# A macaron decoder layer: two more q/k products by Strassen's scheme, and wider transfers for each attention head

## The reference

```
h = x + 0.5 * SwiGLU_1(rmsnorm(x))
u = rmsnorm(h)
[xp | q | k | v | gate_logits] = u @ w_in       # 512 | 512 | 512 | 512 | 2048 columns
y_pool = causal_pool_mixer(xp) @ w_branch_pool  # 4 groups of 128 channels, windows 2, 4, 8, 16
y_sb = stick_breaking_attention(q, k, v) @ w_branch_attn   # 8 heads of 64, no softmax
m = sigmoid(g_pool) * y_pool + sigmoid(g_sb) * y_sb
h = h + m @ w_out
h = h + 0.5 * SwiGLU_2(rmsnorm(h));  out = rmsnorm(h)
```

## Time and profile before

| | |
|---|---|
| runs | 1937.56, 1937.66, 1938.7 us (median 1937.66) |
| profiled execution, first to last instruction (span) | 1937.1 us; the median is 0.56 us above it |
| busy PE / PEld / DVE / ACT / POOL | 1923.7 / 1607.4 / 1338.3 / 772.0 / 136.9 us |
| mean granted PE clock | 0.999 of full speed |
| mean DMA rate | 179 GB/s |

### The profile page before, as it was taken

How to read it: one execution, slowest core, us unless ns; L and a number is a source line. 1 busy time by engine, 2 the same in 40 slices (tenths; PEclk the granted TensorE clock), 3 DMA queues, 4 the chain that set the end, 5 groups by cost and what they waited for, 6 DMA issues and landing times.

```text
span 1937.1 us, 25171 instructions
## 1 busy us (share of the span) xinstructions
PE 1923.7 (99%) x9094; PEld 1607.4 (83%) x9094; DVE 1338.3 (69%) x1656; ACT 772.0 (40%) x1154; POOL 136.9 (7%) x218
## 2 busy tenths in 40 slices
PE   9999999999999999999999999999999999999998
PEld 9888888888888888888888888888888888888887
DVE  6987777775566667425777778789767776755655
ACT  7423232333434424214565652464323232324344
POOL 1000000000000100002333320010000000000002
PEclk9999999999999999999999999999999999999999
DMA  5456645468676503546645347643535454677665
GB/s 163 148 202 229 226 160 164 171 219 309 201 237 194 179 24 103 177 152 190 164 131 161 108 148 249 206 143 109 183 132 187 149 184 139 221 262 241 206 192 204
DMA packets 245092, 347.20 MB, mean 179 GB/s; under 512 B 16144, under 2 KB 150032, under 8 KB 240400
## 3 DMA queue, kind: packets, MB, share of 16 engines
q1 hardware_dynamic: 245008, 346.09, 54.9%
HBM read 232.79 MB, written 112.98 MB: 178 GB/s over the span
## 4 chain that ended last, share of the span: by engine, by line
PE 55%; DVE 2%; DMA 1%; issue 1%; ACT 1%; SPq 0%; POOL 0%; POOLq 0%; DVEq 0%; ACTq 0%
PE bank L1091 20%; PE bank L1188 12%; PE bank L1135 4%; PE bank L1137 4%; PE bank L1136 4%; PE bank L1047 2%; PE bank L1257 2%; PE bank L1285 2%; PE bank L1349 2%; DMA dn_lo_raw<-act_dram 1%; PE bank L1366 1%; PE bank L1365 1%; PE bank L1336 1%; PE bank L1334 1%; DVE tail_p L2471 0%
## 5 line engine op out<-in xcount | busy, mean ns | idle before, releaser
L1905 DVE TENSOR_TENSOR dn_lo<-dn_lo_raw,dn_hi 128x1024 fp32r<-128x1024 f32 x149 | 181.8, 1224 | 151.6 <-ACT dn_hi L1545 151.2
L1091 PE MATMUL bank<-hi_t,wa_hi 128*128 128x512 f32 x640 | 249.1, 389 | 0.2 <-issue 0.2
L1091 PE MATMUL bank<-hi_t,wa_lo 128*128 128x512 f32 x640 | 249.0, 389 | 0.0
L1091 PE MATMUL bank<-lo_t,wa_hi 128*128 128x512 f32 x640 | 249.0, 389 | 0.0
L1545 ACT ACTIVATE dn_hi<-dn_lo_raw 128x1024 fp32r<-128x1024 f32 x149 | 158.0, 1061 | 217.6 <-DMA dn_lo_raw<-act_dram 217.6
L1135 PE MATMUL bank<-dn_hi 128*128 128x512 f32 x596 | 232.7, 390 | 0.6 <-DVE dn_lo L1905 0.6
L1136 PE MATMUL bank<-dn_hi,dn_lo 128*128 128x512 f32 x596 | 231.9, 389 | 0.0
L1137 PE MATMUL bank<-dn_lo,dn_hi 128*128 128x512 f32 x596 | 231.9, 389 | 0.0
L1091 PE MATMUL bank<-hi_b,wa_hi 128*128 128x512 f32 x480 | 186.9, 389 | 0.5 <-DVE up L2029 0.5
L1091 PE MATMUL bank<-lo_b,wa_hi 128*128 128x512 f32 x480 | 186.8, 389 | 0.0
L1091 PE MATMUL bank<-hi_b,wa_lo 128*128 128x512 f32 x480 | 186.7, 389 | 0.0
(11 more groups left out here) (237 smaller groups left out, 3555.3 us busy)
## 6 DMA issues: line engine op xcount, KB each, us to landing
wa_lo_raw<-in_ffn_w_gate_up_dram SPq DMA_DIRECT2D x87, 512.0 KB, 5.0
dn_lo_raw<-act_dram SPq DMA_DIRECT2D x149, 256.0 KB, 4.3
act_dram<-g SPq DMA_DIRECT2D x44, 512.0 KB, 4.5
wd_t<-in_ffn_w_down_dram SPq DMA_DIRECT2D x44, 512.0 KB, 6.6
act_dram<-s_of SPq DMA_DIRECT2D x88, 256.0 KB, 6.5
wd_dram<-wd_t SPq DMA_DIRECT2D x22, 1024.0 KB, 6.0
dn_lo_raw<-wd_dram SPq DMA_DIRECT2D x85, 256.0 KB, 3.3
dn_lo_raw<-in_ffn_w_down_dram SPq DMA_DIRECT2D x64, 256.0 KB, 3.0
```

The source lines that it names most:

```text
L1091: last = nc.tensor.matmul(acc, lhs, rhs, start=n == 0 and i != 2 and i < 5, stop=n == 11, skip_group_check=True)
L1905: return nc.vector.tensor_tensor(dst, raw, hi.bitcast(f32), ALU.subtract)
```

## The change

Q and k of head pairs 0 and 1 and both xp units are now made by seven products of 12 matmuls each, in `mix_unit(b)`, in place of four banks of 24. Q and k of pairs 2 and 3 stay as `unit_quad`. All six stand at the front, in the order q/k pair 2, pair 3 (plain), then q/k pair 0, pair 1, xp unit 1, xp unit 0 (mixed units 0 to 3). Values, group products and pool branch follow, and attention comes straight behind the pool branch. The activation sums of the scheme (`tu_*`, four blocks of 128 x 2048) are made once, from `u_hi + u_lo`. The mixed units have their own weight buffers, of which the raw one (`ws_raw`) is single. Q and k go out by a ring of three buffers, 512 KB each for hi and lo. The pool branch's c22 now comes before c11 in unit 0. Its `pool_weight_sums(2)` moves from before c12(0) to after c21(0). A head is loaded by three transfers of 128 rows, and head 0 in two halves of 512 columns. In attention the PSUM banks are renumbered, and `HEAD_SHARE` gives the first step 16 more of the gate matmuls' shares; per step they are [22, 22, 15, 10, 4, ...], before [7, 23, 15, 11, 4, ...], the first 11 ahead of the first logits. Three semaphores are merged into others, the load of ScalarE's sigmoid table moves to before the q/k units, and `down(1)` waits for its banks one pass later.

```diff
+MIX_UNITS = (tuple(("qk", pair) for pair in PAIR_ORDER[2:]) + ... + (("xp", 1), ("xp", 0)))
+HEAD_SHARE = 16
+    shares[0] += HEAD_SHARE
 # PE
+            def mix_unit(b):
+                s = (b + 1) % 2
+                for i in range(7):
+                    place, hi, lo, (kind, slot) = PRODUCTS[i]
...
+                    if b >= 2 and i == 0:
+                        pe.wait_ge(mb_copied, 2 * (b - 2) + 2)
+                    if b >= 2 and i in (1, 3, 4):
+                        pe.wait_ge(mb_add, 5 * (b - 2) + (1 if i == 1 else i + 1))
+                    if i % 2 == 0:
+                        pe.wait_ge(mb_lo, mix_order(b, i // 2))
+                    if b == 0 and i in (2, 3, 4, 6):
+                        pe.wait_ge(rt_lo, {2: 1, 3: 2, 4: 3, 6: 4}[i])
+                    if i == 2:
+                        pe.wait_ge(mb_copied, 2 * b + 1)
+                    if i >= 5:
+                        pe.wait_ge(mb_add, 5 * b + i - 3)
+                    for n in range(12):
...
+                    last.then_inc(mb_prod, 1)
             for m in range(2):
-                unit_quad(U_P[m], U_P[m] % 2, Q_P[m], fresh=m == 0)
+                unit_quad(U_A[m], U_A[m] % 2, Q_A[m], fresh=m == 0)
+            for b in range(NM):
+                mix_unit(b)
+            values(0, range(4))
+            values(1, range(2))
             group_quad(0)
-            values(0, range(NT))
-            values(1, range(4))
+            values(1, range(2, 4))
+            values(0, range(4, NT))
             group_quad(1)
             values(1, range(4, NT))
             for u in range(KT // 2):
                 pool_branch_unit(u)
-            for m in range(4):
-                unit_quad(U_QK + m, (U_QK + m) % 2, Q_QK + m)
 # PE, pool_branch_unit: product 1 runs its six matmuls with w_hi first
-                pe.wait_ge(wlo, U_B + u + 1)
-                        kt, p = n // 3, n % 3
+                        kt, p = (n % 2, n // 2) if i == 0 else (n // 3, n % 3)
+                        if i == 0 and n == 4:
+                            pe.wait_ge(wlo, U_B + u + 1)
 # SP
+            def load_mix(b):
+                if b:
+                    sp_.wait_ge(mb_lo, 4 * b)
...
+            load_mix(1)
+            for b in range(NM - 2):
+                load_mix(b + 2)
+                spill_mix(b, 0)
+                spill_mix(b, 1)
 # SP, load_head
-                for dst, part, cols in ((q_st[top], 0, 0), (q_st[low], 1, 0), (k_hi2[top], 0, SEQ),
-                                        (k_hi2[low], 0, SEQ), (k_lo2[top], 1, SEQ), (k_lo2[low], 1, SEQ)):
-                    sp_.dma_start(dst[:, slot, :].bitcast(f32),
-                                  qk_dram[part, pair, rows, cols:cols + SEQ]).then_inc(head_in[slot], 16)
+                for c0, c1 in ((HALF, SEQ), (0, HALF)) if hn == 0 else ((0, SEQ),):
+                    landed = head_in[slot] if c0 == 0 else half_in
+                    if hn == 0 and c0:
+                        for i in range(3):
+                            sp_.wait_ge(ring_sp[i], 32 * ring_uses(i))
+                        sp_.wait_ge(pool_prod, 6 * (KT // 2 - 1) + 3)
+                    for dst, part in ((k_hi2, 0), (k_lo2, 1)):
+                        sp_.dma_start(dst[:, slot, c0:c1].bitcast(f32),
+                                      qk_dram[part, pair, rows, SEQ + c0:SEQ + c1].unsqueeze(0).broadcast_to([2, 64, c1 - c0])).then_inc(landed, 16)
+                    if hn == 0 and c0:
+                        sp_.wait_ge(pool_prod, 6 * (KT // 2 - 1) + 4)
+                    sp_.dma_start(q_st[:, slot, c0:c1].bitcast(f32), qk_dram[:, pair, rows, c0:c1]).then_inc(landed, 16)
 # DVE
+            def mix_unit(b):
+                if b:
+                    mix_c21(b - 1)
+                    mix_out(b - 1, 1, 0, 4)
+                mix_c11(b)
+                mix_out(b, 0, 0, 1)
+                mix_c22(b, 0)
+                if b + 1 < NM:
+                    mix_weight_sums(b + 1)
+                mix_c22(b, 1)
...
+            split(U_V[0] % 2, U_V[0] + 1, None)
+            mix_c21(NM - 1)
...
             for u in range(KT // 2):
-                if u == 0:
+                if u:
+                    split_static(U_B + u + 1)
                     pool_c11(u)
-                split_static(U_B + u + 1)
-                if u:
+                    pool_c22(u)
+                else:
+                    pool_c22(u)
                     pool_c11(u)
-                pool_c22(u)
-                if u + 2 < KT // 2:
+                    split_static(U_B + u + 1)
+                if u and u + 2 < KT // 2:
                     pool_weight_sums(u + 2)
                 pool_c12(u)
                 pool_c21(u)
+                if u == 0:
+                    pool_weight_sums(u + 2)
 # GpSimd
+            mix_raw(1)
...
+            mix_raw(0)
```

More of the change, by code:

```diff
@@ L90, with tile_of, ring_uses @@
 HEADS = 2 * len(PAIR_ORDER)
+MIX_UNITS = (tuple(("qk", pair) for pair in PAIR_ORDER[2:]) + tuple(("gate", j) for j in range(0, EARLY, 2))
+             + (("xp", 1), ("xp", 0)))
+NM = len(MIX_UNITS)
+FIRST_TILE = 4
+RING_TILES = FIRST_TILE + 2 * (NM - 2)
+RING_AT = tuple((RING_TILES - 1 - i) % 3 for i in range(3))
+RING_LAST = tuple(RING_AT.index(i) for i in range(3))
+def tile_of(b, a):
+    return FIRST_TILE + 2 * b + a
+def ring_uses(slot, before=RING_TILES):
+    return len(range(slot, before, 3))
 def attention_tiles():
@@ L443, in macaron_layer @@
         ms_sum = sem("ms_sum")
-        late_in = [sem(f"late_in{i}") for i in range(3)]
         part_ok = sem("part_ok")
@@ L558, in pool_place @@
         def pool_place(u, b):
-            return pst_odd[:, :] if b == 0 and u % 2 else pst[:, b, :]
+            return pst_even[:, :] if b == 0 and u % 2 == 0 else pst[:, b, :]
         @block.sync
@@ L627, in load_dn @@
                 own = which and e >= LATE
-                into = late_in[e - LATE] if own else dn_in[slot]
+                into = ring_sp[e - LATE] if own else dn_in[slot]
                 if SLOTS <= e and not own:
@@ L1256, in branch_sum @@
                     kt, p = n // 3, n % 3
-                    last = nc.tensor.matmul(bank[:, b, :], weights(w_lo if p == 2 else w_hi, kt),
+                    last = nc.tensor.matmul(bank[:, 4 + b, :], weights(w_lo if p == 2 else w_hi, kt),
                                             (rhs_lo if p == 1 else rhs_hi)(kt), start=n == 0, stop=n == 3 * BR - 1)
@@ L1316, in gate_parts @@
                     cols = slice(th * HALF, (th + 1) * HALF)
-                    last = products(bank[:, fb % 2, :], j % 2, ab, lambda kt: u_hi[:, kt, cols],
+                    last = products(bank[:, 4 + fb % 2, :], j % 2, ab, lambda kt: u_hi[:, kt, cols],
                                     lambda kt: u_lo[:, kt, cols], part=(m, m + 1))
@@ L1681, in take_qk @@
-            def take_qk(m):
-                for b in range(4):
-                    th, ab = b // 2, b % 2
-                    if b == 0 and m >= 2:
-                        act.wait_ge(qk_sp[m - 2], 32)
-                    act.wait_ge(acc_ready, 4 * (Q_QK + m) + b + 1)
-                    c = ab * SEQ + th * HALF
-                    nc.scalar.activation(qk_hi[m % 2][:, c:c + HALF], bank[:, b, :], ACT.Copy,
-                                         scale=1.0 if ab else QSCALE).then_inc(ev_hi, 1)
@@ new lines, in mix_post @@
+            def mix_post(b, a, th, adds):
+                kind = MIX_UNITS[b][0]
+                if kind == "xp":
+                    return
+                act.wait_ge(mb_add, 5 * b + adds)
+                if kind == "gate":
+                    nc.scalar.activation(mix_dst(b, a, th), mix_dst(b, a, th), ACT.Sigmoid).then_inc(mb_post, 1)
+                else:
+                    nc.scalar.activation(ring_hi[tile_of(b, a) % 3][:, th * HALF:(th + 1) * HALF], mix_dst(b, a, th), ACT.Copy,
+                                         scale=1.0 if a else QSCALE).then_inc(mb_post, 1)
```

742 lines of the change are left out of this document (494 added, 248 removed).

## The result

The changed kernel takes **2059.31 us** (median of 4 runs, 2058.2 to 2059.65) against 1938.18 of the kernel before: 1.0625 times as long, 95% interval 1.0612 to 1.0637. The forecast, 1932.7, and its range (1926 to 1941) were wrong; rival C, which had 0.19, is what happened. It cost more than the 2001 that I gave it, within its own ends of 1974 and 2105.

What follows compares the result with a forecast made beforehand. PE was taken to bound the kernel, busy 1923.7 of 1937.1 us. The removed matmuls (-10.9) and the other terms sum to -5.0: span 1932.1, plus 0.56 for the median, 1932.7 us, range 1926 to 1941.

Steps and rivals of the forecast that it cites:

- rival C: Attention: each head's transfer, 2 parts x 64 rows, runs on 2 of 16 DMA engines; +68 us, 2001 us; chance 0.19.
- Entry to attention: Start of attention: head 0's first half lands in 5.6 us, nearly covered by 6.6 to 8 us of PE work; +0.2 us.
- Attention's own matmuls are the same: Attention: matmuls unchanged, stalls fractions of a us that the shares move; 0, ends -1 and +1 us.
- 48 matmuls: Six projection units: 576 matmuls become 528, at 0.2267 us each; -10.9 us.
- stall at 763.80: Pool branch: PE's 0.27 us wait for c22 behind VectorE's split of unit 1's weights goes; -0.3 us.
- entry to the values: First value matmul waits for the value weights' low part, made behind the last mixed unit's c12; +0.5 us.
- pool unit 0, product 6: Pool branch: product 6 waits for c22, which waits for the last value tile's store; +2.0 us.
- pool unit 1, product 3: Pool branch: product 3 waits for ScalarE's copy of product 1, late behind VectorE's moved weight sums; +3.2 us.
- mixed units: Mixed projection units: VectorE's work fits, q/k stores have 0.7 us of slack; +0.3 us, ends 0 and 2.
- activation sums: VectorE and GpSimd adding u_hi + u_lo finish in time; 0, ends 0 and +1 us if VectorE stretches beside GpSimd.
- A: Pool branch: neither stall shows, so the full gain comes, 1927 us; chance 0.14.
- B: Mixed units, pool branch and head 0: slow landings of weights and q/k stores cost +4.5 us, no change, 1937 us; chance 0.13.

Runs made afterwards that it cites:

- a_inter: The changed kernel, still three transfers of 128 rows a head, with rows interleaved so that 64 is outermost in the source: 1934.12 us, 0.9976 of before.
- a_spread: The changed kernel with each head from the third on asked for in six pieces of half the columns, still 2 x 64 rows: 2019.2 us, 1.0415 of before.
- a_six: The changed kernel with heads read as before, six transfers of 64 rows each, head 0 still in two halves: 1934.87 us, 0.9983 of before.
- i_pool: a_inter with pool unit 2's weight sums moved before unit 0's c22, and unit 0's weight split on GpSimd instead of VectorE: 1932.99 us, 0.9970 of before.

## Why the prediction was wrong

**The step that failed** is the pair of terms "Entry to attention ... +0.2" and "Attention's own matmuls are the same ...: 0". They took the head's transfers to land in 5.6 us, the time of six transfers of 64 rows, which is a row of another form of transfer. What the runs showed in its place: the new form moves at 51 to 53 GB/s, attention takes 398.25 us where a_inter, with the same bytes and 64 outermost, takes 272.74: 125.5 us. C had this mechanism, the place and the sign, and I gave it 0.19 because no row of before showed such a transfer. The form of the code alone, 2 x 64, should have weighed more, since nothing in the trace spoke against it, and its price was six times that of the largest term of the sum.

**C's size** was 68 us, measured 125.5. Its rate was right: 27.3 forecast for an engine, 25.5 to 27 measured. In attention of after PE stands 108.5 us, where it stands 2.2 in a_inter, and is busy 289.72 us for the same matmuls, where it is busy 270.55:

- The six heads of the steady part: 46 us forecast, 68.0 measured (the six long waits from 993.90 to 1225.39 us, 46.3 us apart, where I had 41.7 a head). I had PE wait for the head; it waited for stores of gates and attention outputs behind the head.
- Head 0 at the entry: 22 forecast, 22.4 measured. The agreement is partly luck, since I took 31 us for the head where my own rate gives 28.8.
- `pool_y` behind head 1: 17.5 us, not in the forecast.
- The clock, which falls where PE waits: 19.2 us, not in the forecast.

Of C's signs, PE waiting for the heads at each change of head came out only at the entry and in a_spread, and for line 996 the profile gives no time to landing.

**The rest of the sum** held nearly term by term; the kernel a_inter, which is the change without C, has a span of 1932.3 us against my 1932.1, and a median of 1934.12 against my 1932.7. The median is off by more because I added 0.56 us to the span; an execution's time stands some 1.8 us above its own span (1934.18 and 1932.3; after, 2058.2 and 2056.4), and I had set the median of all runs against the span of one. In medians a_inter gains 4.3 us (1938.40 to 1934.12), where the sum had 5.0:

| term | forecast | measured |
|---|---|---|
| 48 matmuls | -10.9 | -10.8 (132.48 to 121.96, less 0.31) |
| stall at 763.80 | -0.3 | -0.3 |
| entry to the values | +0.5 | +0.31 (783.90, where VectorE's split ends at 783.80) |
| pool unit 0, product 6 | +2.0 | +1.66 |
| pool unit 1, product 3 | +3.2 | +2.9, and +1.3 of clock |
| mixed units | +0.3 | +0.1 |
| activation sums | 0 | 0 |
| entry to attention | +0.2 | 0 (a_inter), 0.94 (a_six) |
| attention | 0 | +0.2 (272.50 to 272.74) |
| behind attention | 0 | -0.8 (from its last matmul to the end) |

The two stalls can be followed to the instruction. PE before product 6 of unit 0 and before product 3 of unit 1 in the kernel after (the branch begins at 833.18), with the gap and its releaser:

```profile
841.80 0.50 PE L1428 MATMUL bank<-yp_hi,w_hi 128*128 128x512 f32 x1 [1.66 <-DVE pst L2757]
...
850.48 0.80 PE L1428 MATMUL bank<-yt_hi,w_hi 128*128 128x512 f32 x1 [2.91 <-ACT pst L1986]
```

and VectorE: the last value tile, c22, the first and the last of the four sums:

```profile
838.46 0.41 DVE L2543 TENSOR_TENSOR v_st<-bank,v_st 128x256 fp32r<-128x256 f32 x1
841.05 0.69 DVE L2757 TENSOR_TENSOR pst<-bank,pool_part 128x512 f32<-128x512 f32 x1 [2.18 <-DMA v_dram<-v_st]
...
846.45 0.41 DVE L2707 TENSOR_TENSOR w_raw<-w_raw 128x256 f32<-128x256 f32 x1
...
847.58 0.41 DVE L2712 TENSOR_TENSOR w_raw<-w_raw 128x256 f32<-128x256 f32 x1
```

The tile ends at 838.87, 5.7 us into the branch as forecast; c22 starts at 7.9 as forecast, named the value store's landing; product 6 at 8.6 (forecast 8.8, though its terms, 7.9, 0.7 and 0.06, add up to 8.7). The sums run from 846.45 to 847.99, ending 5.4 us later against the branch's start than before (5.5 forecast); product 3 starts at 850.48, where the forecast had 8.7 us from product 6 and the trace has 8.68. Before, the sums stood ahead of c12 and ScalarE's copy was never late. The forecast's +3.2 covered the gap and left out the clock.

**Contention.** I took a factor of 1.66 from the earlier trace rows. It is no factor: GpSimd's add there ends at 913.39 and VectorE's split, begun at 912.48, ends at 913.94, 0.55 us later, as in i_pool, where VectorE's instruction too ends shortly behind GpSimd's. The same is seen in the activation sums. GpSimd's first sum and VectorE's instructions beside it in the kernel after:

```profile
664.00 4.59 POOL L3004 TENSOR_TENSOR tu_lo_raw<-u_hi,u_lo 128x2048 f32<-128x2048 f32 x1
```

```profile
664.07 5.61 DVE L2166 SCALAR_TENSOR_TENSOR u_lo_raw<-h,rstd,gain 128x1024 f32<-128x1024 f32 x1 [0.99 <-POOL rstd L2989]
669.60 2.47 DVE L2159 TENSOR_TENSOR u_lo<-bank,u_hi 128x512 fp32r<-128x512 f32 x4
```

VectorE's instruction with two operands in SBUF took 5.61 us for 1.27 and ended 1.09 us behind GpSimd's end; the next, which reads PSUM, ran four in 2.47 us, undisturbed by GpSimd's second sum from 669.85 on. It cost PE nothing: no matmul of the mixed units waited 0.2 us or more.

The hold goes both ways. In a_inter's attention GpSimd's add, which takes 1.3 us by itself, began at 1051.39 beside an instruction of VectorE with two SBUF operands that ended at 1053.07, and took 2.78; VectorE's next one then ended 1.08 us behind GpSimd:

```profile
1051.39 2.78 POOL L3033 TENSOR_TENSOR gst<-gst,pool_y 128x512 f32<-128x512 f32 x1 [0.93 <-ACT gst L2108]
```

```profile
1050.78 2.29 DVE L2858 TENSOR_TENSOR_SCAN tail_p<-keep,zero_col 128x1024 f32<-128x1024 f32 x1 [1.26 <-ACT a L2069]
1053.11 2.14 DVE L2862 TENSOR_TENSOR a<-a,tail_p 128x1023 f32<-128x1023 f32 x1
```

In i_pool, too, GpSimd's 5.57 us for what takes 4.59 above fits the 1.1 us that VectorE still ran.

**Rivals A and B.** A's premise, no stall in the pool branch, is not met. B's slow landings in the mixed units did not come: they take 76.6 us for 336 matmuls and the 0.31, where 76.2 is the pace.

## What to carry to other kernels

Before two transfers are merged into one, read the outermost dimension of both sides as the instruction will carry it: a 2 there put 1.57 MB on two of 16 engines, and the same bytes with 64 outermost ran on all. When a wait's named engine had been idle itself, follow its own idle time on to the next releaser, and count the traffic that stands behind a slow transfer as well as the transfer. It was 85.5 of the 108 us of waits here. A stall added to PE can carry a loss of clock as well (1.3 us behind the gap of 2.9), and a mechanism with no row against it and a price above all others deserves a chance by its rule, not by the silence of the trace.

## What the runs showed of the hardware

The number of engines of a transfer went with its outermost dimension: 48 and 64 rows ran as before, 2 x 64 and 62 rows at 51 to 53 GB/s (0.13 of 16 engines busy in the kernel after), 61 rows at 27 (0.07). This is the rule of the Trainium skill ("DMA: Bandwidth & Descriptors", "Why a DMA increments its semaphore by 16 and not by 1"): the largest number up to 16 that divides the slowest dimension of both sides. The runs agree at 2 and 1 by rate and share, and at 16 by the kernel's time. Behind such a transfer the issue of the next on SP took 5.04 us for 256 KB, where it takes 0.6 otherwise.

GpSimd's instruction with two SBUF operands and VectorE's with two held each other back: the one that began second ended a little less than its own time behind the first one's end (VectorE 1.09 us behind GpSimd at 664 and 827 us and 0.55 at 912; at 1051 us in a_inter GpSimd 1.10 behind VectorE). VectorE's instructions that read PSUM ran beside GpSimd's at their own pace (four in 2.47 us). The Trainium skill ("GPSIMD Engine Reference", "Key points") names contention for these operands; the traces agree, and show its size here, up to 4.3 us for one instruction of VectorE.

In the two stretches of 4 us around and behind PE's gap of 2.9 us the granted clock was 0.77 and 0.80 (a_inter, 848 to 856 us). Behind the gap of 1.66 us it was 1.00 (844 to 848 us).
